# Prompt and sample tokens as separate programs, with the expert steps of one placed between the mixer stages of the other

## The reference

```
act  = gelu(u_tab[eidx] . x)                # one dot product of width 1024 per expert
out += gate * act * v_tab[eidx]             # one row of width 1024 per expert
```

## Time and profile before

| what | value |
|---|---|
| runs, median of 3 | 3264.99 us (3261.94 to 3277.42) |
| the profiled execution, its own time | 3268.03 us |
| its span in the trace | 3266.3 us |
| TensorE clock granted, mean | 0.859 of full |
| busy: TensorE, VectorE, ScalarE, GpSimd | 2494.9, 1504.7, 667.9, 994.8 us |
| moved by DMA | 859.83 MB, of which 721.47 MB by indirect gathers |

### The profile page before, as it was taken

How to read it: one execution, slowest core, us unless ns; L and a number is a source line. 1 busy time by engine, 2 the same in 40 slices (tenths; PEclk the granted TensorE clock), 3 DMA queues, 4 the chain that set the end, 5 groups by cost and what they waited for, 6 DMA issues and landing times. The chain is left out here.

```text
span 3266.3 us, 24414 instructions
## 1 busy us (share of the span) xinstructions
PE 2494.9 (76%) x7841; PEld 1308.8 (40%) x7841; DVE 1504.7 (46%) x3672; ACT 667.9 (20%) x1486; POOL 994.8 (30%) x843
## 2 busy tenths in 40 slices
PE   7887846785777777778789778948957778777776
PEld 2362312453332333333357567825623333333333
DVE  0113222215666666766413351151076767666753
ACT  0213434112212221211110221110121212212211
POOL 0000067102444444444200232100034444444441
PEclk9998967797889988988899785569978989988988
DMA  6434378335999999999823103312279999999994
GB/s 224 149 109 168 142 257 290 125 103 200 395 398 412 395 402 393 417 397 396 321 90 119 58 1 107 99 65 77 90 315 400 418 397 403 409 393 403 419 404 169
DMA packets 219178, 859.83 MB, mean 263 GB/s; under 512 B 16492, under 2 KB 98885, under 8 KB 137110
## 3 DMA queue, kind: packets, MB, share of 16 engines
q0 software_dynamic: 102400, 721.47, 55.3%
q1 hardware_dynamic: 116681, 137.21, 12.6%
HBM read 845.50 MB, written 13.18 MB: 263 GB/s over the span
## 5 line engine op out<-in xcount | busy, mean ns | idle before, releaser
L1879 POOL DMA_INDIRECT exp_uv<-in_peer_uv_dram,expert x640 | 765.2, 1196 | 1363.9 <-PE exp_acc L1910 840.2
L1909 PE MATMUL exp_acc<-exp_uv,exp_diag 128*128 128x512 f32 x1280 | 756.4, 676 | 409.0 <-ACT exp_diag L1926 408.8
L1960 DVE CUSTOM_DVE_ANT_0 exp_uv<-exp_uv,htok 128x1024 f32<-128x1024 f32 x640 | 773.1, 1227 | 513.7 <-DMA exp_uv<-in_peer_uv_dram,expert 504.7
L1910 PE MATMUL exp_acc<-exp_uv,exp_diag 128*128 128x512 f32 x1280 | 712.4, 640 | 0.0
L1909 PEld LDWEIGHTS exp_acc<-exp_uv,exp_diag 128*128 128x128 f32 x1280 | 257.2, 212 | 800.7 <-ACT exp_diag L1926 534.1
L1910 PEld LDWEIGHTS exp_acc<-exp_uv,exp_diag 128*128 128x128 f32 x1280 | 269.2, 210 | 358.7 <-issue 358.7
L1918 ACT ACTIVATE exp_act<-exp_dots 128x4 f32<-128x4 f32 x160 | 32.9, 205 | 1198.3 <-DVE exp_dots L1960 1198.3
L1926 ACT ACTIVATE exp_diag<-ident,exp_w 128x128 f32<-128x128 f32 x640 | 201.7, 386 | 0.0
L503 PE MATMUL ssd_in_ps<-hT,ssd_in_w 128*128 128x320 f32 x640 | 175.0, 437 | 10.4 <-ACT hT L400 10.4
L503 PE MATMUL peer_q_ps<-hT,peer_q_w 128*128 128x320 f32 x512 | 143.9, 445 | 20.8 <-ACT hT L400 20.8
L503 PEld LDWEIGHTS ssd_in_ps<-hT,ssd_in_w 128*128 128x128 f32 x640 | 123.0, 192 | 62.5 <-issue 12.7
(11 more groups left out here) (398 smaller groups left out, 2449.1 us busy)
## 6 DMA issues: line engine op xcount, KB each, us to landing
ada_w<-in_ada_w_dram SPq DMA_DIRECT2D x12, 2048.0 KB, 7.5
attp_w<-in_ada_w_dram SPq DMA_DIRECT2D x12, 2048.0 KB, 7.8
ssd_in_w<-in_ssd_w_in_dram SPq DMA_DIRECT2D x20, 1024.0 KB, 5.0
peer_q_w<-in_peer_wq_dram SPq DMA_DIRECT2D x16, 1024.0 KB, 5.2
ab_in_w<-in_ab_w_in_dram SPq DMA_DIRECT2D x10, 1024.0 KB, 4.8
exp_uv<-in_peer_uv_dram,expert POOLq DMA_INDIRECT x640, 9.3
out_ssm_sample_dram<-state_hd SPq DMA_DIRECT2D x8, 1024.0 KB, 4.5
ssd_out_w<-in_ssd_w_out_dram SPq DMA_DIRECT2D x4, 2048.0 KB, 7.5
```

What stands on the lines that cost most here:

```text
L1879: pool.indirect_dma_start(slot(g)[:], None, table, bass.IndirectOffsetOnAxis(ap=experts[:, g:g + 1], axis=0)).then_inc(landing(g)[0], 16)
L1909: pe.matmul(acc[t % 2][0][:], diag[g % (2 * GRP)][:], slot(g)[:, D:D + 512], start=False, stop=False, skip_group_check=True)
L1910: pe.matmul(acc[t % 2][1][:], diag[g % (2 * GRP)][:], slot(g)[:, D + 512:2 * D], start=False, stop=False, skip_group_check=True).then_inc( ...
L1960: dve.tensor_tensor_reduce(slot(g)[:, 0:D], slot(g)[:, 0:D], m.htok[:, t, :], 1.0, 0.0, ALU.mult, ALU.add, dots[:, i % 2, k:k + 1]).then_i ...
```

## The change: what it does

The prompt (256 columns) and the sample (64 columns) become separate programs (`PROMPT`, `SAMPLE`) that share the engines. Only setup, `ada`, `ab_in`, pooling remain common. The stages from `ab_out` on exist twice, with 64 or 256 moving columns, and load their weights twice. `stage_experts` becomes a class `Experts` whose work on each engine is cut into steps, one per group of four gathers, which other stages can call: the sample has 16 groups (17 steps) per layer, the prompt 64 groups (65 steps). `Beside` spreads a number of steps over the places of a stage. What has not been called by then runs in `rest()`, a block of steps alone. The order of `build` and the numbers of steps:

```diff
+RINGS = (6, 9, 5, 12)
...
+    stage_pool(nc, m, a)
+    stage_attend_sample(nc, m, a)
+    stage_project(nc, m, "ab_out_s", a["ab_w_out_pk"], SAMPLE, m.yT[:, :, TP:T], residual=mod[:, 2 * KC:3 * KC, :])
+    s0 = peer_head(nc, m, a, 0, SAMPLE, held)
+    s0.begin(RINGS[0])
+    stage_attend_prompt(nc, m, a, steps=10)
+    held.give("proj_ab")
+    stage_project(nc, m, "ab_out_p", a["ab_w_out_pk"], PROMPT, m.yT[:, :, 0:TP], residual=mod[:, 2 * KC:3 * KC, :], steps=2)
+    held.give("y_ab")
+    p0 = peer_head(nc, m, a, 0, PROMPT, held, 4, 1)
+    s0.rest()
+    s0.end()
+    p0.begin(RINGS[1])
+    mixer_ssd(nc, m, a, SAMPLE, held, (11, 3, 3, 6, 2, 3))
+    s1 = peer_head(nc, m, a, 1, SAMPLE, held, 3, 1)
+    p0.rest()
+    p0.end()
+    s1.begin(RINGS[2])
+    mixer_ssd(nc, m, a, PROMPT, held, (6, 2, 4, 0, 1, 2))
+    p1 = peer_head(nc, m, a, 1, PROMPT, held, 2, 0)
+    s1.rest()
+    s1.end()
+    p1.begin(RINGS[3])
+    stage_norm_out(nc, m, SAMPLE)
+    stage_out(nc, m, a, SAMPLE)
+    p1.rest()
+    p1.end()
+    stage_norm_out(nc, m, PROMPT)
+    stage_out(nc, m, a, PROMPT)
```

```diff
+class Beside:
+    def __init__(self, m, places, steps):
+        self.x = m.beside
+        self.due = [(k + 1) * steps // places - k * steps // places for k in range(places)] if self.x else [0] * places
...
+    def pool(self, pool):
...
+        lo = 0 if i == 0 else (i - 1) * GRP + self.ring
+        table = self.a["peer_uv"].rearrange("l e d -> (l e) d")
+        for g in range(lo, min(i * GRP + self.ring, self.n_all)):
...
+            if g >= self.ring:
+                pool.wait_ge(self.mixed, g - self.ring + 1)
+            pool.indirect_dma_start(self.slot(g)[:], None, table,
+                                    bass.IndirectOffsetOnAxis(ap=self.expert[:, g:g + 1], axis=0)).then_inc(self.landing(g)[0], 16)
...
+    def act(self, act):
...
+        if self.ring < 2 * GRP and i:
+            self.spread(act, i - 1)
+        if i < self.groups:
...
+            act.wait_ge(self.dotted, (i + 1) * GRP)
+            act.activation(self.act4[:, i % 2, :], self.dots[:, i % 2, :], ACT.Gelu).then_inc(self.acted, 1)
+        if self.ring >= 2 * GRP and i:
+            self.spread(act, i - 1)
...
+    def dve(self, dve):
...
+        if self.ring < 2 * GRP and i:
+            self.weigh(dve, i - 1)
+        if i < self.groups:
...
+                dve.wait_ge(sem, there)
+                dve.tensor_tensor_reduce(self.slot(g)[:, 0:D], self.slot(g)[:, 0:D], self.htok[:, t, :], 1.0, 0.0, ALU.mult, ALU.add,
+                                         self.dots[:, i % 2, k:k + 1]).then_inc(self.dotted, 1)
+        if self.ring >= 2 * GRP and i:
+            self.weigh(dve, i - 1)
```

`pool`, `act` and `dve` are methods of `Experts`, and i counts the steps called. `best_sums` or `experts_of` stands at the end of VectorE's step where one is due. TensorE's step i is the matmuls of group i - 1. In `stage_project` the steps of a block stand ahead of that block on each engine:

```diff
             def _(pe):
+                for i in range(blocks):
+                    by.pe(pe, i)
+                    pe.wait_ge(loaded[i % 2], i // 2 * 16 + 16)
...
             def _(dve):
+                for i in range(blocks):
+                    by.dve(dve, i)
```

More of the change, by code:

```diff
@@ L337, in _ @@
             def _(sp):
-                with sp.Fori(0, Ada.STEPS) as i:
+                for i in range(Ada.STEPS):
                     for k in range(2):
@@ L465, in stage_project @@
+def stage_project(nc, m, name, w, part, src, out=None, kcn=KC, bw=256, residual=None, norm=None, after=None, conv=None, steps=0):
+    n, per, blocks = part.n, bw // P, w.shape[0]
+    x = m.xT[:, :, part.cols]
+    wide = per * n > 512
+    with Stage(nc, m, name) as s:
+        wt = [s.sb(f"w{i}", [P, kcn, bw]) for i in range(2)]
         tmp = s.sb("part", [P, TS])
-        ps = [[s.bank(f"ps{i}{j}") for j in range(2)] for i in range(2)]
+        ps = [[s.bank(f"ps{i}{j}") for j in range(per if wide else 1)] for i in range(2)]
@@ L473, in stage_project, with into @@
+        def into(o, k):
+            return out[:, o:o + k, :] if after is None or o < XC else after[:, o - XC:o - XC + k, :]
         with nc.Block() as block:
@@ new lines, in _ @@
+            @block.scalar
+            def _(act):
+                if norm:
+                    norm.scalar(act)
+                for i in range(blocks):
+                    by.act(act, i)
+                    if residual is None and wide:
+                        for j in range(per):
+                            act.wait_ge(made, i * per + j + 1)
+                            act.copy(into(i * per + j, 1), ps[i % 2][j][:, 0:n].unsqueeze(1)).then_inc(taken, 1)
+                    elif residual is None:
+                        act.wait_ge(made, (i + 1) * per)
+                        act.copy(into(i * per, per), ps[i % 2][0][:, 0:per * n].rearrange("p (j n) -> p j n", n=n)).then_inc(taken, per)
@@ L1674, in stage_scores @@
         hkept = s.sem("h_kept")
-        cleared = s.sem("qz_cleared")
+        by = Beside(m, 1, steps)
+        sets = [(t, g) for t in range(1 if sample else 2) for g in range(2 if sample else 4)]
+        rows = [(t, g) for t in range(1 if sample else 2) for g in range(2)]
         with nc.Block() as block:
@@ L1947, in _ @@
[L1947 to L1948 removed]
+                while self.i_act <= self.groups:
+                    self.act(act)
             @block.vector
             def _(dve):
[L1952 to L1961 removed]
@@ L1985, in _ @@
-                choice.best_sums(dve, 1)
-                choice.experts_of(dve, 1)
-                groups = turns * per
-                for i in range(groups):
-                    j, k = i // per, i % per
-                    dot(i)
-                    if i:
-                        weigh(i - 1)
-                    if j + 2 < turns and k == 0:
-                        choice.best_sums(dve, j + 2)
-                    if j + 2 < turns and k == 1:
-                        choice.experts_of(dve, j + 2)
-                    for t in (1, 2):
-                        if i == first[t] * per + 3:
-                            end(t - 1)
```

1700 lines of the change are left out of this document (936 added, 764 removed).

## The result

The changed kernel takes 3915.5 us (median of 4 runs, 3914.0 to 3930.5) against 3271.2 us of the kernel before in the same session. The ratio is 1.198, 95% interval 1.193 to 1.203: slower, as forecast, but by 644 us where the forecast had 375. It lies 85 us above the upper end of the range.

The account below looks back on a forecast made before the run. Gathers' DMA was taken to bound the expert stages (1717 us), TensorE or latency chains most of the other 1549 us. Split stages 1676 us plus steps 1964 us gave 3640 us, range 3370 to 3830.

Parts of the forecast that it names:

- the circle of the ring of nine: Prompt's layer 0 steps: three late gathers wait for group i - 1, behind the dots of group i; 16.3 us per step.
- the price of a thin instruction: Sample's projections: an instruction with 64 columns costs 0.125 us, its other end 0.185 us at half clock.
- The split: All stages run separately for prompt and sample, without any step: 1676 us against 1549, costing 127 us.
- The steps: Expert steps of both layers, beside other stages and alone: 1964 us in sum, against 1717.
- Five slots beside the prompt's mixer: Sample's 17 steps in layer 1: 10 in projections at 7.5 us, 7 in latency chains at 14, together 173 us.
- The 32 steps beside the sample's mixer: Prompt's layer 0 steps: 11 in `ssd_in` add 120 us, the other 21 cost 11.5 us each; together 361 us.
- Six slots in the attention: Sample's layer 0 steps in the prompt's attention: 10 x 12.3 us for two late gathers, plus 27 for choices, 150 us.
- The last 64 groups: Prompt's layer 1 on ring 12, alone as before: 64 x 10.66 = 682 us.
- Hidden beside the mixer: Rival: mixer work fills the cycle, so all 66 steps beside something cost TensorE's 8.1 us; 3430 us, chance 0.12.
- Faster: Rival: slots refill fast enough to keep the DMA busy with nine, period under 12 us; 3200 us, chance 0.15.
- Slower still: Rival: TensorE drops to half clock in thin stages, 92 us in sample projections, some 60 in first gathers; 3790 us, chance 0.07.
- The queues taking turns: Steps beside sample projections: a gather meeting a load takes up to 2.6 us more, some 45 us, 3685 in all.

Follow-up runs that it names:

- the run without steps: The changed kernel with all step counts zero, so every step runs in the blocks of steps alone, rings and order kept: 4261.7 us.
- early order: Changed kernel with `weigh` and `spread` of group i - 1 ahead of the dots of group i in the ring of nine too: 3571.6 us.
- the best version: Changed kernel with weights ahead of dots, 64 of the prompt's first steps beside, slots 8, 9, 6, 12, and 128 columns in the sample's normed projections: 3413.1 us.
- late order: `weigh` and `spread` of group i - 1 behind the dots of group i, as in the changed kernel (3915.5 us); the kernel before with nine slots took 4409.0 us.

## Why the prediction was wrong, point by point

The direction, the circle of the ring of nine and its rank as the largest single loss were right, and so were its signs: 17.7 us per step, a DMA share of 0.60, and 222 us in `ssd_in_s` where 215 was forecast. What failed are the sizes of two kinds of terms, by 272 us of the span in all: the price of a thin instruction in stages that stand alone, and what a step costs beside a stage. With the run without steps, each term can be set beside its measurement.

**The split, forecast 1676 us.** By stages without steps: `ada` 83 (forecast 74), prompt's attention 124 (131), prompt's head of layer 0 129 (129), prompt's projections of layer 1 316 (321), middle of the mixer 174 for the sample (179) and 151 for the prompt (155). Norm and output, twice, took 38 (48). These are fine. The first step that failed is the price of a thin instruction: "with 64 columns an instruction costs what a small one costs, 0.125 us". It costs 0.214. Sample's head of layer 0: 117 us (forecast 88); its projections of layer 1: 146 + 61 + 64 and 19 of scores = 290 (forecast 197). That is 122 us in two terms. The forecast named the other end, 0.185 us at half clock, and left it to a rival with a chance of 0.07. The row behind 0.185 was the one that resembled the case (few columns in a row at a granted clock of 0.50); 0.125 came from 16 instructions of 64 columns in 2.00 us at full clock. The shape was right and the clock was not. And 0.185 was no bound either.

In the kernel after itself the 0.214 stands only in layer 0's head, which has no steps (29 us above the forecast). In layer 1 steps stand between the thin instructions, and they cost 0.129 us in `ssd_in_s` and 0.153 in the two other projections, 86 us less than alone. So the forecast's price nearly held there, and the 93 us of layer 1 move to the steps: the 350 us below are a difference to stages that ran at half clock. By whole stages, steps included and counted from the stages' own starts, the kernel after against the forecast reads: sample's head of layer 0 117 (88), prompt's attention and head of layer 0 494 (470), sample's layer 1 808 (737), prompt's first steps alone 584 (538), prompt's layer 1 710 (649), last steps 721 (682), `ada` 87 (74), norm and output 37 (48). Most of the miss is in stages with steps.

The Trainium skill (TensorE: Matmul & The Clock Gate, Why this matters for your kernels) says that keeping TensorE continuously busy brings it to the full clock, and that a thin matmul should have its loop ordered so that no load is waited for within it, or be padded. The first does not hold here: busy for 140 of 146 us at 0.50. Padding does help, by 49 us in `ssd_in_s` with 128 columns, and not with 256.

**The steps, forecast 1964 us.** Measured, as the stage after less the stage alone:

| | forecast | measured |
|---|---|---|
| sample, layer 0, ring 6 | 210 | 243 |
| prompt, layer 0, 32 beside | 361 | 350 |
| prompt, layer 0, 33 alone | 538 | 577 |
| sample, layer 1, ring 5 | 173 | 243 |
| prompt, layer 1, alone | 682 | 717 |

The two sides, 1776 us by the stages above (with the 354 that did not change) and 2130 us by this table, meet the span of 3912 to within 6 us.

- *Nine slots alone: 17.5 us, forecast 16.3.* The legs were right in kind. In the turn shown the first late gather goes out 5.1 us after the dots, not 4.4: the granted clock was 0.50 to 0.52 from the group's start until 2106 and 1.00 after it. The late gathers land 3.4 and 2.9 us apart instead of 2.6, though they went out only 2.1 and 1.7 us apart; so TensorE's pace does not explain this part, and no run settles what does. This turn adds up to 18.1 us, the upper end that was named.
- *Five slots beside the prompt's mixer: +70.* Here a second step failed: "TensorE goes on for two blocks of 7.2 us, and the step costs its own work, 8.1 us". In `ssd_in_p` a step costs 73 / 6 = 12 us. TensorE's timeline there:

```profile
2537.74 9.61 PE L2132 MATMUL exp1s_acc<-exp1s_uv,exp1s_diag 128*128 128x512 f32 x16 [5.20 <-ACT exp1s_diag L2175]
2547.19 27.79 PE L573 MATMUL ssd_in_p_ps<-hT,ssd_in_p_w 128*128 128x256 f32 x128
2580.10 8.83 PE L2132 MATMUL exp1s_acc<-exp1s_uv,exp1s_diag 128*128 128x512 f32 x16 [5.12 <-ACT exp1s_diag L2175]
```

  and its waits there (us in total, times, longest):

```profile
PE exp1s_acc L2132 <- ACT exp1s_diag L2175: 21.9, 5, 5.4
```

  The first of the six steps has no matmuls, so there are five groups. TensorE reaches them and stands there for the diagonals, 1.0 us ahead of the first and 5.1 to 5.4 us ahead of each of the other four. `weigh` and `spread` are placed with the same block on VectorE and ScalarE, behind those engines' taking of the block before, so they start when TensorE is already there. This is read from the timelines; no run moved them. The forecast let VectorE wait but not TensorE. In convolution and scan the steps cost 109 / 6 = 18 us, the full period of five slots.
- *The 32 steps beside the sample's mixer: 350, forecast 361.* In `ssd_in_s` a step comes to (222 - 146) / 11 = 6.9 us, less than TensorE's own 8.1, since the steps also lift the clock of the stage's own instructions. The other 21 come to 13 us each, where the forecast let up to 8 us of mixer work fit into the waiting and took 11.5.
- *Six slots in the attention: 18.3 us per step, forecast 15.* Eight slots gave 13.3 (in the early order, which these steps have in both runs), so the late gathers are 5 us of each.
- *The last 64 groups: 717, forecast 682.* They run at 389 GB/s in the middle where the kernel before has 401 to 405, some 4%. The old program keeps two sets of accumulators and turns a tile while the next one runs. The new one has one set, and at the tile's change TensorE stands for the next diagonals:

```profile
3544.47 15.71 PE L2132 MATMUL exp1p_acc<-exp1p_uv,exp1p_diag 128*128 128x512 f32 x30 [7.45 <-ACT exp1p_diag L2175]
```

  Start, change and tail are shared by 64 groups instead of 80. What lowered the rate of the DMA itself was not tried.

**The rivals.** *Hidden beside the mixer*: no; a step beside the sample's mixer costs 350 / 32 = 10.9 us, not 8.1. *Faster*: its point was a period under 12 us in the rest, and the trace has 17.5. The advice of the Trainium skill behind it (Perfetto Trace Analysis, Optimization Strategy), that interleaving phases with different limits may improve the time, holds within the split program: 315 us from 3830 to 3515. What it does not pay for is the split, some 220 us (1770 against 1549), and shorter rings. *Slower still* (3790): this was the nearest number, and its half clock is there in the thin stages without steps; it deserved to be part of the forecast's sum. In the thin stages with steps it is not what came. *The queues taking turns*: in `ssd_in_s`, once the first nine were in, the gathers landed in 7.9 us in the median (8.1 in the mean), and in 7.7 (7.4) in the rest without weight loads. So up to 0.7 us per gather shows, and not 2.6. Weight loads did lengthen, in `ssd_in_s` from 4.8 to 8.1 us, hidden by the second buffer.

Of the loss of some 645 us, the order (with nine slots) accounts for 344. Taking the other half of the steps beside, longer short rings and the wide columns bring 158 more. 143 us remain with the best version.

## What to carry to other kernels

A ring's length and the order of the streams are one decision. With N slots and groups of G, write out which group's release the last gather of group i waits for; with nine slots and groups of four it is group i - 2. If that release stands behind the dots of group i - 1 in the program, as here in the late order, the period is the whole chain, whatever the engines' busy times. Cutting a batch in two costs more than the moved columns say: in a stage of their own, with 128 stationary columns, 64 moving columns took nearly as long as 256, and 128 were a third faster than either. Time such a stage both alone and with the other work in it: the same 64 columns cost 0.214 us alone and 0.129 between steps.

## What the runs showed of the hardware

- TensorE busy for 96% of 146 us with 64 moving columns per instruction was granted 0.50 of its clock throughout. The same stage with 128 columns was granted 0.93. Being busy did not bring it the full clock here.
- Thrown-away work made a kernel faster: 87 us of 3830 by doubling the moved columns of 3 stages. Beside the steps' wide matmuls the same edit gained nothing in `ssd_in_s`: the granted clock there was already 0.87, and 64 and 128 columns both cost 0.120 us per instruction.
- Steps alone on nine slots were granted 0.74 in the late order, and in the early order 0.92 in one run and 0.85 in another. In the cycle of nine slots TensorE started its groups after waits of 7 to 10 us and took 8.5 to 10.1 us for each; in the prompt's last steps a group that started after a wait of some 1 us took 7.1. So a cycle of waits costs twice, once as waiting and once as a slower TensorE that lengthens the waiting.
